# An expert layer's down matrices issued by ScalarE's DMA queue, the gate/up matrices by SyncE's

## The chip, the cores and the metric

The kernel runs on one core of one Trainium2 chip, in float32 throughout. The metric is the device time of one launch in microseconds (us). The engines are TensorE (PE; PEld is its weight load), VectorE (DVE), ScalarE (ACT), GpSimd (POOL) and SyncE (SP, which here only issues DMAs). All DMAs of the core run on its 16 DMA engines; the profile tells them apart by queue: q1 is SyncE's, q10 ScalarE's, q0 GpSimd's.

## What is computed

One decoder layer on 1024 tokens of width 1024: three token mixers, a norm, then a mixture of 64 experts (each token goes to 8 of them) with one shared expert and a per-layer embedding, then a last norm. The change lies in the routed experts, which the reference writes as

```python
def swiglu(x, w_gu, w_down):
    gate, up = jnp.split(x @ w_gu, 2, axis=-1)
    return (jax.nn.silu(gate) * up) @ w_down

def block(acc, inp):
    tok, wt, ex = inp
    y = swiglu(x_pad[tok], w_gu[ex], w_down[ex])
    return acc.at[tok].add((y * wt[:, None]).astype(acc.dtype)), None
```

`w_gu[ex]` is 1024 x 512 (2 MB), `w_down[ex]` is 256 x 1024 (1 MB). `tok` are the tokens routed to the expert.

## The kernel before

The experts are sorted by load, and the 63 most loaded ones get one *place* each (NS = 63; the rest goes through a spill loop at the end). Table `rank_e`, computed on the chip, says which expert stands at a place. A place holds 128 rows (a **single**) or more, up to 216 (a **double**, whose rows above 128 are a second block); in `PLACES` doubles and singles mostly take turns, 34 and 29 of them. `chunks(r)` counts the blocks ahead of place r.

What happens for place r, by engine:

- GpSimd (L3392 to L3402): in turn r it gathers the rows of place r (4 DMAs for the first block, one for each 32 rows of the second, and one of gates for each block; helper line L3343), then issues the adds of place r - 4 (`add_place`, L3359): an indirect DMA for each block that adds the output rows into `acc_scratch` in HBM. An add waits until all adds of earlier places have landed (x_out). A gather waits for the transpose (x_xt) and the gate columns (x_gate) of the places up to two back.
- VectorE (L3260 to L3277): transposes the gathered rows (L3175), multiplies gate and up (L3269, L3272), writes one half of the output (L3237, or L3231 for a second block of at most 32 rows) and copies the gate columns (L3245, L3248).
- TensorE (L2703 to L2727): `hidden(r + 1)`, the gate/up product (L2647 for a double, L2690 for a single), comes before the down product of place r (L2655, and L2662 or L2670 for a second block). A single also has its hidden block turned (L2697), one place before its down product.
- ScalarE (L2832 to L2848): the Silu of place r (L2841), the outputs of place r - 1 (`y_half`, L2821 and L2823), and for a single the copy of the turned hidden block (L2848), on which its down product waits.
- SyncE (L2420 to L2423): the weight loads. `gu` and `dn` are rings of RING = 5 buffers each. `gate_up_in(r)` waits until place r - 5's gate/up product is done (x_u), `down_in(r)` until place r - 5's down product is (x_dn). Both look the expert up with `table`, which reads it into a register. All stand in one queue, in program order:

```python
for r in range(3, NS):
    gate_up_in(r)
    if r >= 4:
        down_in(r)
```

`outputs(r)` needs the adds of place r - 2 landed, since `yoA` and `yoB` have two buffers each. The down product of place r + 1 needs the outputs of place r, since both use the same PSUM banks.

Of the kernel before, what the change touches and what calls it, by code (L numbers as in the profile page):

```python
# [24 lines left out]
NE = 64  # L25
# [3 lines left out]
RING = 5  # L29
# [64 lines left out]
def place_rows(q):  # L94

    return rank_rows(PLACES[q])
# [74 lines left out]
def build(nc, a, out):  # L171

    ctx = ExitStack()
    with ctx:
        stage_sems = []

        def sem(name):
            stage_sems.append(nc.alloc_semaphore(name=name))
            return stage_sems[-1]
# [16 lines left out]
        def carve(n, at=None):  # L196
            at0 = top[0] if at is None else at
            if at is None:
                top[0] += n
            assert at0 + n <= ARENA, (at0, n)  # L200
            return A[:, at0:at0 + n]
# [1897 lines left out]
        with nc.Block() as block:  # L2099
# [25 lines left out]
            def _(pool):  # L2125
# [10 lines left out]
            rank_e = take(NE).bitcast(I32)  # L2136
# [54 lines left out]
                  for x, at in ((1, E_SPILL), (2, E_SPILL + 4 * CQ), (4, R3 + 4 * HALF))}  # L2191
# [3 lines left out]
            NS = NE - 1  # L2195
            gu = [carve(GU, at).rearrange("p (k n) -> p k n", k=KD) for at in (E_GU, base, base + GU, hT_at, hT_at + GU)]
            dn = [carve(DN, at).rearrange("p (f n) -> p f n", f=2) for at in [E_GU + GU] + [AC + i * DN for i in range(RING - 1)]]
# [27 lines left out]
            e_par, e_lg, e_sc, e_chain, e_g, e_st, e_msk, e_tot, e_cnt, e_rank, e_cap, e_cols, e_rows, e_tab, e_pos = (  # L2225
                sem("e_" + n) for n in ("par", "logits", "scores", "chain", "gates", "store", "mask", "totals", "count", "rank",
                                        "capacity", "cols", "rows", "tables", "pos"))
# [27 lines left out]
            x_wg, x_wd = ([sem(f"x_w{n}{i}") for i in range(RING)] for n in "gd")  # L2255
# [27 lines left out]
            dn_v = a["exp_w_down"].rearrange("e (f p) n -> e p f n", p=P)  # L2283
# [13 lines left out]
            def more(r):  # L2297
                return place_rows(r) - P
# [11 lines left out]
            def chunks(r):  # L2310

                return sum(2 if more(q) else 1 for q in range(r))

            def pair(r):
                return 2 * (r % 3)

            def singles(r):

                return sum(not more(q) for q in range(r))

            def table(eng, ap, i, most):
                return eng.value_load(ap[0:1, bass.ds(i, 1)], min_val=0, max_val=most)

            def n_spills(eng):
                return eng.value_load(spills[0:1, 0:1], min_val=1, max_val=OVB)
# [14 lines left out]
            def _(sp):  # L2340
# [38 lines left out]
                def gate_up_in(r):  # L2379
                    e = table(sp, rank_e, r, NE - 1)  # L2380
                    if r == 0:
                        sp.wait_ge(f_dn, 2 * NT)
                    elif r == 1:
                        sp.wait_ge(f_p7, 7 * PPAIRS)
                    elif r < RING:
                        sp.wait_ge(f_p7, 7 * PU)
                        if r >= 3:
                            sp.wait_ge(f_sg, KEPT)
                    else:
                        sp.wait_ge(x_u, r - RING + 1)  # L2390
                    sp.dma_start(two_rows(gu[r % RING]), gu_v[bass.ds(e, 1)].rearrange("a p c two n -> p (a c) (two n)")).then_inc(x_wg[r % RING], 16)

                def down_in(r):
                    e = table(sp, rank_e, r, NE - 1)
                    if 0 < r < RING:
                        sp.wait_ge(f_st[r - 1], 32)
                    elif r:
                        sp.wait_ge(x_dn, chunks(r - RING + 1))
                    sp.dma_start(dn[r % RING], dn_v[bass.ds(e, 1)].rearrange("a p f n -> p (a f) n")).then_inc(x_wd[r % RING], 16)
# [19 lines left out]
                        down_in(t // 2)  # L2419
                for r in range(3, NS):  # L2420
                    gate_up_in(r)
                    if r >= 4:
                        down_in(r)  # L2423
                sp.wait_ge(x_u, NS - RING + 1)
                sp.dma_start(n_g, row("ln2_g", 0, D)).then_inc(n_par, 16)
# [3 lines left out]
                n = n_spills(sp)  # L2429
                with sp.Fori(0, n) as j:  # L2430
                    e = table(sp, spill_e, j, NE - 1)
# [333 lines left out]
            def _(act):  # L2765
# [28 lines left out]
                for q in range(4):  # L2794
                    half, f = q // 2, q % 2
# [20 lines left out]
                def y_half(r, out, gate, n, c, bank):  # L2816
                    act.wait_ge(x_gate, c + 1)
                    if r >= 2:
                        act.wait_ge(x_out, 16 * chunks(r - 1))
                    act.wait_ge(x_dn, c + 1)  # L2820
                    last = nc.scalar.activation(out[r % 2][0:n, 0:HALF], PS[0:n, bank, :], ACT.Copy, scale=gate[r % 2][0:n, :])  # L2821
                    if n <= 32:
                        last = nc.scalar.activation(out[r % 2][0:n, HALF:2 * HALF], PS[64:64 + n, bank, :], ACT.Copy,  # L2823
                                                    scale=gate[r % 2][0:n, :])
                    last.then_inc(x_ya, 1)

                def outputs(r):
                    y_half(r, yoA, gateA, P, chunks(r), 6)
                    if more(r):
                        y_half(r, yoB, gateB, more(r), chunks(r) + 1, pair(r))  # L2830

                for r in range(NS):  # L2832
                    n = place_rows(r)
                    if more(r):
                        act.wait_ge(x_g, r + 1 - singles(r))
                    else:
                        act.wait_ge(x_u, r + 1)
                    if r >= 2:
                        act.wait_ge(x_hid, r - 1)
                        act.wait_ge(x_ht, singles(r - 1))  # L2840
                    nc.scalar.activation(sl[r % 2][:, 0:2 * n], PS[:, pair(r), 0:2 * n], ACT.Silu).then_inc(x_sl, 1)  # L2841
                    if r:
                        outputs(r - 1)
                    if not more(r):
                        act.wait_ge(x_ht, singles(r) + 1)
                        if r >= 2:
                            act.wait_ge(x_dn, chunks(r - 1))
                        nc.scalar.activation(hidT[r % 2][:, 0:2 * P], PS[:, pair(r) + 1, 0:2 * P], ACT.Copy).then_inc(x_hc, 1)  # L2848
                outputs(NS - 1)
                n = n_spills(act)  # L2850
# [641 lines left out]
```

## Time and profile before

| | |
|---|---|
| median of 3 runs | 2307.42 us (2306.7 to 2308.29) |
| profiled execution, its own time | 2311.8 us |
| its span, first to last instruction | 2310.0 us |
| TensorE busy | 2243.6 us, 97% |
| VectorE, ScalarE, GpSimd busy | 1165.2, 459.6, 757.2 us |
| mean granted clock of TensorE | 0.992 |
| DMA | 386.12 MB, mean 167 GB/s; 345 to 361 GB/s in the expert stage |

The span is what lies between the first and the last instruction; 1.8 us of the execution's own time lie around it. The expert stage takes the last third, from about 1440 to 2270. A busy share says how much of the time an engine had work in hand. For TensorE it counts matmuls whose ends are modelled, so a wait can be larger than the gaps that it leaves. A DMA share near or above 1 says that packets were always under way on all 16 engines.

### The profile page before, as it was taken

Reading aid. Unit: us, or ns where it says so; the run is one execution under the profiler, and the core shown is the slowest. Engines: PE = TensorE matmul, PEld = TensorE weight load, DVE = VectorE, ACT = ScalarE, POOL = GpSimd, SP = SyncE. Lnnn points to the kernel's source line nnn. Section 1 sums busy time; section 2 is a strip of 40 time slices with the busy share of each in tenths; the row PEclk is TensorE's granted clock in tenths of the full one; section 3 lists DMA queues with packets and bytes.
Section 4 is the critical chain, followed back from the end, with each engine's and each line's share of the span. In section 5 each row is a group of like instructions: output and inputs, shape, how many; then the busy total and the mean of one; then the engine's idle time right before and its main releaser. Section 6 shows DMA issues by size and latency. Waiting matters only on the chain. (4 is left out here: it accounts for less than half of the span.)

```text
span 2310.0 us, 26726 instructions
## 1 busy us (share of the span) xinstructions
PE 2243.6 (97%) x9622; PEld 1314.9 (57%) x9622; DVE 1165.2 (50%) x2023; ACT 459.6 (20%) x778; POOL 757.2 (33%) x755
## 2 busy tenths in 40 slices
PE   8999999999999999999999999999999999999985
PEld 4784554445795444444445567665656666566552
DVE  6643886786757454554585556323223222232324
ACT  3001114665441111011102100111111111111113
POOL 1000110002531000000000056567777677776652
PEclk9999999999999999999999999999999999999998
DMA  7212011113001111101322320899999999999985
GB/s 295 79 38 72 3 35 60 49 43 110 2 30 64 55 61 58 55 28 55 148 98 99 134 74 1 308 361 358 355 354 358 346 345 349 350 349 347 346 236 179
DMA packets 142389, 386.12 MB, mean 167 GB/s; under 512 B 22508, under 2 KB 51424, under 8 KB 141234
## 3 DMA queue, kind: packets, MB, share of 16 engines
q1 hardware_dynamic: 110242, 307.49, 36.0%
q0 software_dynamic: 30976, 70.08, 12.0%
q10 hardware_dynamic: 1040, 6.83, 0.7%
q8 instruction: 78, 1.28, 0.2%
q14 instruction: 53, 0.43, 0.1%
HBM read 328.30 MB, written 66.58 MB: 171 GB/s over the span
## 5 line engine op out<-in xcount | busy, mean ns | idle before, releaser
L3343 POOL DMA_INDIRECT arena<-hp_scratch,arena x300 | 305.4, 1018 | 143.0 <-issue 85.3
L2647 PE MATMUL banks<-arena 128*128 128x136 f32 (+8 forms) x2240 | 305.7, 297 | 2.7 <-DVE arena L3286 1.9
L2647 PEld LDWEIGHTS banks<-arena 128*128 128x128 f32 x2240 | 301.3, 190 | 6.1 <-issue 3.9
L1887 PE MATMUL banks<-arena 128*128 128x512 f32 x672 | 290.8, 592 | 2.5 <-DVE arena L2020 1.5
L2655 PE MATMUL banks<-arena 128*128 128x512 f32 (+1 forms) x528 | 238.9, 595 | 5.6 <-ACT arena L2848 4.7
L1887 PEld LDWEIGHTS banks<-arena 128*128 128x128 f32 x672 | 127.2, 190 | 163.0 <-issue 162.5
L2690 PE MATMUL banks<-arena 128*128 128x512 f32 x464 | 204.8, 593 | 0.0
L3237 DVE TENSOR_SCALAR arena<-banks,arena 128x512 f32<-128x512 f32 (+4 forms) x75 | 56.3, 751 | 289.1 <-DMA acc_scratch<-arena 247.5
L285 POOL TENSOR_SCALAR arena<-arena 128x1 f32<-128x1 f32 x16 | 4.9, 307 | 567.6 <-DVE arena L276 567.6
L3359 POOL DMA_INDIRECT acc_scratch<-arena x97 | 150.4, 1551 | 81.1 <-DMA acc_scratch<-arena 39.5
L3175 DVE STREAM_TRANSPOSE arena<-arena 128x1024 f32<-128x1024 f32 (+3 forms) x97 | 96.7, 1001 | 156.5 <-DMA arena<-gt_scratch,arena 156.0
L2655 PEld LDWEIGHTS banks<-arena 128*128 128x128 f32 (+1 forms) x528 | 97.9, 189 | 117.2 <-issue 111.0
L2821 ACT ACTIVATE arena<-banks,arena 128x512 f32<-128x512 f32 (+7 forms) x97 | 62.8, 680 | 491.1 <-DMA acc_scratch<-arena 402.8
L1131 PE MATMUL banks<-arena 128*128 128x512 f32 x336 | 150.7, 604 | 3.7 <-ACT arena L1346 3.7
L2690 PEld LDWEIGHTS banks<-arena 128*128 128x128 f32 x464 | 87.4, 189 | 113.6 <-issue 113.6
L1899 PE MATMUL banks<-arena 128*128 128x512 f32 x336 | 146.3, 592 | 0.0
L449 PE MATMUL banks<-arena 128*128 128x256 f32 (+1 forms) x560 | 145.1, 421 | 0.0
L2031 DVE TENSOR_TENSOR arena<-arena,banks 128x512 f32<-128x512 f32 x84 | 56.5, 687 | 164.3 <-PE banks L1887 164.3
L449 PEld LDWEIGHTS banks<-arena 128*128 128x128 f32 x560 | 106.0, 189 | 39.0 <-issue 26.8
L1131 PEld LDWEIGHTS banks<-arena 128*128 128x128 f32 x336 | 63.8, 193 | 88.7 <-issue 83.1
L1899 PEld LDWEIGHTS banks<-arena 128*128 128x128 f32 x336 | 63.6, 189 | 80.7 <-issue 80.7
L3343 POOL DMA_INDIRECT arena<-gt_scratch,arena x98 | 96.0, 979 | 29.9 <-issue 24.7
(477 smaller groups left out, 2983.1 us busy)
## 6 DMA issues: line engine op xcount, KB each, us to landing
arena<-in_exp_w_gu SPq DMA_DIRECT2D x64, 2048.0 KB, 30.2
arena<-in_exp_w_down SPq DMA_DIRECT2D x64, 1024.0 KB, 26.3
arena<-in_w_in SPq DMA_DIRECT2D x20, 1024.0 KB, 5.4
arena<-in_w_in SPq DMA_DIRECT2D x6, 2048.0 KB, 8.5
arena<-in_w_branch SPq DMA_DIRECT2D x12, 512.0 KB, 6.5
arena<-in_ple_w_g SPq DMA_DIRECT2D x3, 2048.0 KB
hp_scratch<-arena SPq DMA_DIRECT2D x10, 512.0 KB, 3.3
acc_scratch<-arena SPq DMA_DIRECT2D x10, 512.0 KB, 4.6
```

Source lines behind the costliest of these rows:

```text
L449: last = nc.tensor.matmul(PS[:, 4 + n % 4, 0:width], lhs(k), rhs(k), start=(k == 0), stop=(k == 3))
L1131: last = nc.tensor.matmul(PS[:, q_bank(n), :], w[:, k, :], tok[:, k, :], start=(k == 0), stop=(k == 3))
L1887: last = nc.tensor.matmul(PS[:, g % 4, :], lhs[:, k, :], rhs[:, k, :], start=(k == 0), stop=(k == 3))
L1899: last = nc.tensor.matmul(PS[:, 4 + g % 4, :], lhs[:, k, :], rhs[:, k, :], start=(k == 0), stop=(k == 1))
L2031: nc.vector.tensor_tensor(dst, src, PS[:, (7 * i + idx) % 4, :], ALU.add).then_inc(m_dve, 1)
L2647: last = nc.tensor.matmul(PS[:, bank + part, f * n:(f + 1) * n], weights[:, k, part * FF + f * P:part * FF + (f + 1) * P], x[:, k, 0:n], s ...
L2655: last = nc.tensor.matmul(PS[0:n, bank + j, :], hid[:, f, lo:lo + n], weights[:, f, j * HALF:(j + 1) * HALF], start=(f == 0), stop=(f == 1))
L2690: last = nc.tensor.matmul(PS[:, pair(r), :], x[:, k, :], gu[r % RING][:, k, :], start=(k == 0), stop=(k == KD - 1))
L2821: last = nc.scalar.activation(out[r % 2][0:n, 0:HALF], PS[0:n, bank, :], ACT.Copy, scale=gate[r % 2][0:n, :])
L3175: nc.vector.transpose(x, src).then_inc(x_xt, 1)
L3343: nc.gpsimd.indirect_dma_start(out=rows[0:n, :], out_offset=None, in_=table, in_offset=bass.IndirectOffsetOnAxis(ap=at, axis=0), bounds_ch ...
L3359: nc.gpsimd.indirect_dma_start(out=acc_d, out_offset=bass.IndirectOffsetOnAxis(ap=slot_i[0:n, block:block + 1], axis=0), in_=rows[0:n, :], ...
```

## The change

SyncE keeps the down loads of the first five places. From place 5 on each is issued by ScalarE, right after it has written its part of the outputs of place r - 5 (whose down product is the last reader of the buffer), with a look-up and a wait of its own on the same count x_dn. The gate/up loads stay where they are. Buffers, sizes, semaphores and what TensorE waits for are unchanged.

```diff
                 for r in range(3, NS):
                     gate_up_in(r)
-                    if r >= 4:
+                    if r == 4:
                         down_in(r)
...
+                def down_in(r):
+                    e = table(act, rank_e, r, NE - 1)
+                    act.wait_ge(x_dn, chunks(r - RING + 1))
+                    act.dma_start(dn[r % RING], dn_v[bass.ds(e, 1)].rearrange("a p f n -> p (a f) n")).then_inc(x_wd[r % RING], 16)
+
+                act.wait_ge(e_tab, 1)
                 for r in range(NS):
...
                     nc.scalar.activation(sl[r % 2][:, 0:2 * n], PS[:, pair(r), 0:2 * n], ACT.Silu).then_inc(x_sl, 1)
                     if r:
                         outputs(r - 1)
+                        if r - 1 + RING < NS:
+                            down_in(r - 1 + RING)
                     if not more(r):
                         act.wait_ge(x_ht, singles(r) + 1)
```

## Rows read from the trace of the kernel before

**Rows 1.** Windows of the expert stage: us, busy us of each engine, PEclk, DMA share, GB/s.

```profile
1480.00:1860.00 380.00, 380.00 (x1702) 244.88 (x1702) 107.15 (x177) 51.93 (x97) 264.11 (x239) 1.00 1.03 358
1860.00:2240.00 380.00, 376.28 (x1743) 237.24 (x1741) 111.89 (x189) 56.18 (x107) 263.49 (x236) 1.00 1.01 339
```

**Rows 2.** TensorE's waits, 1440 to 2270: who waited for whom, us, times, longest.

```profile
PE banks L2655 <- ACT arena L2848: 4.7, 2, 4.5
PE banks L2697 <- DVE arena L3272: 3.6, 3, 2.4
```

**Rows 3.** Chain of waits, 2028 to 2130, shares of that stretch by line.

```profile
by line: DMA acc_scratch<-arena 70.9%; issue 18.3%; POOL arena L3343 10.3%; POOL acc_scratch L3359 4.3%; DVE arena L3237 1.5%; POOLq L3343 0.4%; POOLq L3359 0.3%; DVE arena L3248 0.1%; POOLq L3372 0.1%; DVE arena L3245 0.1%; DVEq L3245 0.1%
```

**Rows 4.** Timeline of GpSimd, 2060 to 2130: start, us, what, [idle before <-releaser].

```profile
2076.37 1.64 POOL L3359 DMA_INDIRECT acc_scratch<-arena  x1 [0.30 <-issue]
2078.31 1.35 POOL L3359 DMA_INDIRECT acc_scratch<-arena  x1 [0.31 <-issue]
...
2087.28 1.62 POOL L3359 DMA_INDIRECT acc_scratch<-arena  x1 [0.99 <-DMA acc_scratch<-arena]
2091.47 1.04 POOL L3343 DMA_INDIRECT arena<-hp_scratch,arena  x1 [2.57 <-DVE arena L3248]
...
2100.54 1.63 POOL L3359 DMA_INDIRECT acc_scratch<-arena  x1 [0.30 <-issue]
```

**Rows 5.** Timeline of VectorE, two stretches: 1795 to 1840 and 2060 to 2130.

```profile
1829.34 0.75 DVE L3237 TENSOR_SCALAR arena<-banks,arena 128x512 f32<-128x512 f32 x1 [3.04 <-PE banks L2655]
...
2086.52 0.75 DVE L3237 TENSOR_SCALAR arena<-banks,arena 128x512 f32<-128x512 f32 x1 [5.18 <-DMA acc_scratch<-arena]
...
2096.49 0.75 DVE L3237 TENSOR_SCALAR arena<-banks,arena 128x512 f32<-128x512 f32 x1 [4.12 <-DMA acc_scratch<-arena]
```

**Rows 6.** Timeline of TensorE and ScalarE around 1836 and 2090.

```profile
1835.91 3.59 PE L2655 MATMUL banks<-arena 128*128 128x512 f32 x8
...
2083.00 8.01 PE L2647 MATMUL banks<-arena 128*128 128x144 f32 x64
2090.84 3.60 PE L2655 MATMUL banks<-arena 128*128 128x512 f32 x8
...
2106.33 8.87 PE L2647 MATMUL banks<-arena 128*128 128x160 f32 x64
...
2088.54 0.38 ACT L2848 ACTIVATE arena<-banks 128x256 f32<-128x256 f32 x1
...
2096.54 0.69 ACT L2821 ACTIVATE arena<-banks,arena 128x512 f32<-128x512 f32 x1 [7.32 <-DMA acc_scratch<-arena]
```

**Rows 7.** Timeline of SyncE's queue around 1560, 2063 and 2083.

```profile
1560.43 0.38 SPq L2399 DMA_DIRECT2D arena<-in_exp_w_down  x1
1561.58 0.38 SPq L2391 DMA_DIRECT2D arena<-in_exp_w_gu  x1
...
2063.52 3.51 SPq L2391 DMA_DIRECT2D arena<-in_exp_w_gu  x1
...
2083.00 4.77 SPq L2399 DMA_DIRECT2D arena<-in_exp_w_down  x1
```

**Rows 8.** Line L2391, all 63 gate/up loads, us from issue to landing.

```profile
DMA to landing us min/median/max: 9.3/30.2/33.0
```

**Rows 9.** ScalarE's earlier DMA L1956, and its queue's packets from 859.4 to 861.9.

```profile
L1956 ACTq DMA_DIRECT2D arena<-y_lru_scratch x1: 403/403/403, 859.5 to 859.5; - x1
...
q10 hardware_dynamic: 3, 0.05, 5.2%
```

**Rows 10.** DMA queues from 2081.2 to 2085: packets, MB, share of 16 engines.

```profile
q0 software_dynamic: 125, 0.51, 67.2%
q1 hardware_dynamic: 138, 0.54, 37.3%
```

**Rows 11.** DMA queues from 14.6 to 19.0.

```profile
q1 hardware_dynamic: 236, 0.90, 52.0%
q10 hardware_dynamic: 235, 0.90, 50.6%
```

## The prediction, made before the changed kernel was run

> **What bounds the kernel now.** I read the page first: TensorE is busy 97% of the span, and over its last 820 us the DMA row stands at 9. That is the stage of the 63 expert places, which the change touches. The windows [rows 1] show both limits at once: of the 760 us from 1480 to 2240 TensorE is busy 756.3, and the DMA share is 1.03, then 1.01. Nothing here has room, and little can be won: the stage's waits [rows 2] hold 4.7 us before L2655 and 3.6 us before L2697 that came through ScalarE or VectorE, 8.3 us in all.
>
> Next, who is nearest behind TensorE. In the chain of waits of a late stretch [rows 3] 70.9% is the landing of the adds into acc_scratch and no weight load appears. So I took one turn of that loop apart [rows 4, 5]. The adds of a double place are issued at 2076.37 and 2078.31; 8.2 us after the second, at 2086.52, they have landed and the outputs of two places later may be written; at 2091.47, the gate columns ready, the next double's seven gathers begin; then the next double's add goes out at 2100.54. One turn (two places) lasts 24.17 us. TensorE itself, from one double's first matmul to the next one's, needs 23.3, from 2083.00 to 2106.33 [rows 6]. In this late part the loop is the slower of the two, and hardly hidden. At 1829.34 VectorE's output waited for TensorE and not for an add [rows 5], so up to there TensorE set the pace. The single place's add between (2087.28, landed 2096.49) has 4.05 us to spare before 2100.54.
>
> The weights are not late: the gate/up load issued at 2063.52 (place 52) lands at most 33.0 us later, 2096.5 [rows 7, 8], and its first matmul runs at 2106.33 [rows 6]: 9.8 us to spare. Down matrices have more.
>
> **The change, part by part.**
> *ScalarE gains 58 issues* (places 5 to 62). Each is a table load into a register, a wait and a DMA. SP shows the load's price: the down issue ends at 1560.81, the gate/up issue starts at 1561.58 with its wait long met, 0.77 us; the issue takes 0.38 when the queue has room [rows 7], and ScalarE's own earlier one took 0.40 [rows 9]. Together 1.15 us, 67 us over the stage, on an engine busy some 14% of it [rows 1]. The wait (x_dn) has been met by the outputs just before, so it costs nothing and nothing new queues behind it. What stands behind the issue is the copy L2848 for a single place and the Silu L2841. The copy ended at 2088.92 and its matmuls began at 2090.84 [rows 6]: 1.9 us of cover, 0.8 after. Not on the path: 0. Without that cover it is 1.15 us each time. On SP an issue took 4.77 us at 2083.00 [rows 7], late in the stage, where at 1560 it took 0.38: I read this as a queue with loads piled up in it. ScalarE's queue would hold one or two loads of 1 MB, so I take 0.38; the ends are 0.37 and 4.8.
>
> *SP loses the same 58* and with them the wait for the down product before each gate/up load, which can then be issued some 4 to 6 us earlier (a down product, 3.6 us, and an issue). It lands 9.8 us early already: 0. The buffers, bytes and other queues' orders stay.
>
> *The down loads move to a third queue.* This is the part that counts. Where adds and SP's queue are both at work [rows 10] they carry 125 and 138 packets: they alternate. By their shares an add packet takes 3.8 x 16 x 0.672 / 125 = 0.327 us and a weight packet 0.164. In the one dense stretch where SP's and ScalarE's queues are both full [rows 11] it is 236 to 235. So I expect three queues to alternate too, which no stretch of this trace shows. A block of 128 rows gives each of the 16 engines 8 add packets: 8 x 0.491 = 3.9 us now, 8 x 0.655 = 5.2 us beside two weight queues, **1.3 us more**, 1.5 with the second block's one or two packets. That is the upper end for one landing; the lower is 0, if they never meet. (The Trainium skill, DMA: Bandwidth & Descriptors, section on queues, rings and completion order, says that each engine goes round-robin between the queue rows that have work, a packet at a time. It speaks against this change: two full weight rows leave the adds a third. For two rows the trace agrees.)
>
> When do they meet? ScalarE ends the single place's output at 2097.2, loads and issues until 2098.4; data started 2.4 us after ScalarE's earlier issue (three packets by 861.9) [rows 9], so at about 2100.4. 1 MB is 16 packets for each engine: 5.2 us beside SP's queue, some 6.6 with the gathers' packets between, so until 2107. The double's adds issued at 2076.37 were moving data in 2081.2 to 2085 [rows 10], 4.8 us after the issue; the ones issued at 2100.54 then from 2105.3. They meet for 1.7 us: about one packet less, 0.4 us. The other down load, after the double's output at 2086.5, falls fully on the single's add: 1.3 us of its 4.05 us to spare, but it moves that place's output and so the first load later by 1.3: up to 3 us of meeting, 0.75. I take 0.6 us for each pair of places. From 1829 to 2240 there are 411 / 24.2 = 17 pairs: 17 x 0.6 = **10 us**. Before that TensorE's pace and the loop's own room absorb it.
>
> *Order among the weights.* The down loads, no longer behind 2 MB, land about 15 us earlier against their use; that is 1.2 MB taken from the gate/up loads, which need 2 MB in 12.2 us: some 7 of their 9.8 us to spare. 0, but a bound: with all gone, it costs.
>
> Sum: 2310.0 span + 1.8 around it = 2311.8 for the profiled execution; plus 10 is 2321.8. The median is 4.4 below that execution: **2317.4 us**, own range 2312.5 to 2325.
>
> **Rivals.**
> *A, the full third.* The down loads cover the double's adds wholly (data later than I think, or packets arriving in bunches). Then each pair costs 1.5 us, 26 us from 1829 on, and the loop overtakes TensorE sooner: of the 14 pairs from 1490 to 1829, each with room of its own that no row fixes (between 0 and 1.5 us, I take 0.5), 14 x 1.0 is 14, less 5 us that TensorE can be kept from its outputs before it notices (ready at 1830.1, wanted at 1835.91 [rows 5, 6]): 9 more. 2307.4 + 35 = 2342. For it: rows 10, 11. Against it: the instants above.
> *B, nothing.* The loads fall between the adds, or the engines are so full that it is all one. (The Trainium skill, same page, section "Issuing engines are not separate DMA queues": all queues end on the same 16 engines, and spreading saves only the sequencer's issue time. By that alone the time stays.) 2307.4, within 4.6. For it: bytes are unchanged and SP's issue time was on no path.
> *C, faster.* If SP's queue, rid of a third of its bytes, runs dry while a double's adds move data, they go at 0.327 instead of 0.491 us: 1.3 us less a turn. It decides once gate/up loads land in under some 12 us instead of 30.2 [rows 8]. TensorE then sets the pace and only the waits of rows 2 can be won: 2307.4 - 8.3 = 2299 at best, 2302 likely. Against it: DMA share above 1 [rows 1], and a queue relieved only of what runs beside it.
> *D, ScalarE stalls.* The issue takes 2 to 4.8 us as on SP. From 1.9 us of cover it decides; some 1 us per pair on the way to the single's down product: 2307.4 + 17 = 2324. Against it: a nearly empty queue. That the change does not do what it says I exclude: order and waits are in the code.
>
> **Numbers.** Forecast 0.43, A 0.14, B 0.28, C 0.10, D 0.05. A measurement here can tell 0.2%, 4.6 us, from no change. Slower: forecast, A and D, 0.62, less 0.02 of the forecast's lower edge; same 0.30; faster 0.10. The range 2302 to 2338 leaves out most of A above and half of C below, about 0.18.
>
> **What would show it.** Right: in the changed profile the double's adds land 0.4 to 1.5 us later than 8.2; a turn of the loop lasts 24.7 or more; ScalarE's issues take 0.4 us; gate/up issues on SP short and early, landing near 30 us or later; down loads landing in about 10; TensorE idle some 10 us more. Wrong: adds landing as before (B), waits of TensorE on gate/up loads (their order was worth more than I gave it), or shorter add landings (C).

## The result, and the profile after

| | before | after |
|---|---|---|
| median | 2307.86 us (4 runs, 2306.7 to 2308.95) | 2331.75 us (4 runs, 2328.6 to 2333.51) |
| ratio after / before | | 1.0103, 95% interval 1.0091 to 1.0116 |
| span of the profiled execution | 2310.0 us | 2331.5 us |

The change costs 24 us. The forecast was slower by 10 (2317.4, range 2302 to 2338): the direction and the resource were right, the size was not.

The edit moves the lines below it: L2841 is now L2847, L2848 is L2856, L3175 is L3183, L3237 is L3245, L3272 (a single's multiplication) is L3280, L3343 is L3351, L3359 is L3367. The down loads of ScalarE stand at L2835.

In three of the five series of runs below even the kernel before took 2336 to 2356 us, so each run is compared only with runs of the kernel before from its own series.

**Where the time went.** The expert stage is cut here by places: from the gate/up product of place 5 to that of 25, 41 and 61. The windows of the kernel before (us, PE, PEld, DVE, ACT, POOL busy; then granted clock, DMA share, GB/s):

```profile
1530.70:1780.60 249.90, 249.90 (x1116) 160.49 (x1115) 72.00 (x119) 35.50 (x66) 177.00 (x160) 1.00 1.03 354
1780.60:1974.90 194.30, 193.50 (x904) 122.91 (x903) 57.27 (x95) 27.07 (x52) 140.85 (x127) 1.00 1.03 350
1974.90:2216.60 241.70, 238.78 (x1116) 152.28 (x1115) 72.63 (x123) 37.14 (x70) 169.50 (x153) 1.00 1.01 338
```

and the same places in the changed kernel:

```profile
1529.30:1790.60 261.30, 253.99 (x1117) 163.62 (x1116) 70.87 (x119) 35.02 (x66) 174.54 (x157) 0.99 1.02 345
1790.60:1990.30 199.70, 195.17 (x904) 124.16 (x903) 57.16 (x95) 27.51 (x52) 141.91 (x129) 0.99 1.02 340
1990.30:2238.20 247.90, 239.73 (x1117) 152.32 (x1116) 72.53 (x123) 37.41 (x70) 170.47 (x154) 1.00 0.97 320
```

The three stretches take 261.3, 199.7 and 247.9 us where they took 249.9, 194.3 and 241.7: **11.4, 5.4 and 6.2 us more**, 23.0 in all. The first 20 places, where I had put nothing, pay half. TensorE idles 7.3 us there (261.30 less 253.99) where it idled none.

The loss does not grow evenly inside these stretches. The forecast's own dividing line was 1829, where place 29's product starts. Cut there, before and then after:

```profile
1530.70:1829.00 298.30, 298.30 (x1374) 194.54 (x1373) 86.99 (x144) 42.80 (x80) 212.36 (x192) 1.00 1.03 354
1829.00:2216.60 387.60, 383.88 (x1759) 241.14 (x1758) 114.91 (x193) 56.90 (x108) 274.99 (x247) 1.00 1.01 343
```

```profile
1529.30:1843.50 314.20, 304.03 (x1375) 198.96 (x1374) 85.85 (x144) 42.57 (x80) 212.74 (x192) 0.98 1.02 342
1843.50:2238.20 394.70, 384.86 (x1760) 241.14 (x1759) 114.71 (x193) 57.37 (x108) 274.17 (x247) 1.00 0.99 329
```

It is **15.9 us up to place 29 and 7.1 after it**. Place by place it comes in steps: from place 11 to 27 the start of the product slips by 15.8 us, from place 27 to 40 by nothing (both kernels take the same time for each), and from 40 to 56 by 6.8 more.

**What TensorE waits for.** From 1480 to 2260, the kernel after, us in total, times, longest (before: [rows 2]):

```profile
PE banks L2697 <- DVE arena L3280: 13.5, 9, 3.2
PE banks L2647 <- issue: 4.0, 3, 2.9
PE banks L2655 <- ACT arena L2856: 2.5, 2, 1.3
```

No wait is for a weight load. (The 4.5 us wait of [rows 2] stands at 2244.6, behind the stretches; its like in the kernel after lies beyond 2260.) The largest kind is the turn of a single's hidden block, L2697, which is late because VectorE's multiplication is. The waits put down to "issue" have a cause too: each of the three ends 0.10 us after VectorE has transposed the rows of that product, the longest at 1804.36, so they are waits for late gathers:

```profile
1803.65 0.71 DVE L3183 STREAM_TRANSPOSE arena<-arena 128x512 f32<-128x512 f32 x1 [2.52 <-DMA arena<-gt_scratch,arena]
1804.46 7.77 PE L2647 MATMUL banks<-arena 128*128 128x176 f32 x41 [2.86 <-issue]
```

One step behind, from 1530 to 1790, VectorE's outputs in the kernel before waited for

```profile
DVE arena L3237 <- DMA acc_scratch<-arena: 63.8, 14, 8.0
...
DVE arena L3237 <- PE banks L2655: 21.7, 8, 3.0
```

and in the kernel after for

```profile
DVE arena L3245 <- DMA acc_scratch<-arena: 120.8, 20, 9.2
```

ScalarE's outputs the same: 13 waits for adds and 10 for TensorE's down product before, 20 for adds and none for TensorE after. The outputs, and with them the whole ring of adds and gathers, now run behind the adds from the start.

**One such delay, followed.** GpSimd, VectorE and TensorE of the kernel after around place 10 (start, us, what, idle before):

```profile
1602.74 1.62 POOL L3367 DMA_INDIRECT acc_scratch<-arena  x1 [2.08 <-DMA acc_scratch<-arena]
1604.84 1.04 POOL L3351 DMA_INDIRECT arena<-hp_scratch,arena  x1 [0.47 <-issue]
...
1614.01 0.96 POOL L3351 DMA_INDIRECT arena<-gt_scratch,arena  x1 [0.30 <-issue]
```

```profile
1613.41 0.75 DVE L3245 TENSOR_SCALAR arena<-banks,arena 128x512 f32<-128x512 f32 x1 [5.63 <-DMA acc_scratch<-arena]
...
1621.14 0.71 DVE L3183 STREAM_TRANSPOSE arena<-arena 128x512 f32<-128x512 f32 x1 [2.01 <-DMA arena<-gt_scratch,arena]
1621.77 0.38 DVE L3280 TENSOR_TENSOR arena<-arena,banks 128x256 f32<-128x256 f32 x1
```

```profile
1618.01 1.04 PE L2670 MATMUL banks<-arena 128*8 128x512 f32 x8
1622.21 0.44 PE L2697 MATMUL banks<-arena 128*128 128x128 f32 x2 [3.16 <-DVE arena L3280]
```

The add of the single place 7 had to wait for the adds ahead of it and went out at 1602.74 (in the kernel before, where it waited for no add, at 1598.20). Eight gathers of 1.3 us each stand behind it, the last from 1614.01. VectorE transposes these rows at 1621.14 and multiplies only behind that, so the hidden block is ready at 1622.15, and TensorE has stood still for 3.16 us. The next windows of the same trace:

```profile
1619.00:1622.20 3.20, 0.05 (x4) 0.00 (x0) 1.15 (x3) 0.00 (x0) 2.59 (x3) 1.00 1.05 349
1622.20:1626.20 4.00, 3.99 (x16) 3.99 (x17) 0.00 (x0) 0.00 (x0) 2.48 (x3) 0.60 1.05 313
1626.20:1630.00 3.80, 3.80 (x24) 3.80 (x23) 0.75 (x1) 1.33 (x3) 0.63 (x1) 0.97 0.98 365
```

After the wait the granted clock is 0.60 for 4 us: it fell to half, the 1.2 GHz level, for most of them, and 4 x 0.40 = 1.6 us more are lost. In the expert stage this happens at the waits of 3.16, 2.61 and 2.86 us near 1622, 1714 and 1804, with 0.91 over each 20 us around them, 1.8 us each. A wait of 2.43 us at 2126.2 was followed by 1.00. So places 5 to 24 add up: 7.3 idle + 2 x 1.8 of clock = 10.9 of the 11.4 us.

**Why the adds are late.** The queues while an add of a single place lands, in the kernel before from 1603 to 1607 (packets, MB, share of the 16 engines):

```profile
q0 software_dynamic: 140, 0.53, 64.5%
q1 hardware_dynamic: 157, 0.63, 40.8%
```

and in the kernel after from 1608 to 1612:

```profile
q0 software_dynamic: 114, 0.43, 52.2%
q1 hardware_dynamic: 116, 0.45, 29.4%
q10 hardware_dynamic: 93, 0.37, 22.6%
```

Each engine sends GpSimd's packets at one in 4 x 16 / 140 = 0.457 us before and one in 0.561 after. Eight packets of a block take 3.7 us before and 4.5 after, 0.8 more. The three queues take nearly equal numbers, as the prediction expected of them; it is also what the Trainium skill, DMA: Bandwidth & Descriptors, section on queues, rings and completion order, says of an engine's queue rows.

Over many places: from the start of the issue of a place's last add to the start of the output it holds up (two places later, only where that output waited for it), medians in us:

| kernel | doubles 5-24, 25-40, 41-59 | singles 5-24, 25-40, 41-59 |
|---|---|---|
| before | 8.97, 9.12, 9.24 | 9.44, 9.41, 9.38 |
| after | 9.54, 8.58, 9.53 | 10.62, 9.73, 10.24 |

A single's add is 1.2, 0.3 and 0.9 us later, a double's 0.6, -0.5 and 0.3. (In the kernel before only three outputs waited for a single's add in places 5 to 24.) Over places 25 to 40 the two together are no later than before, and there nothing is lost from place 27 on.

**The loads.** The gate/up loads (L2391) and ScalarE's down loads (L2835) of the kernel after, from issue to landing, and their issues:

```profile
L2391 SPq DMA_DIRECT2D arena<-in_exp_w_gu x63: 372/373/7074, 1356.7 to 2198.8; - x63
...
DMA to landing us min/median/max: 8.9/15.4/41.0
```

```profile
L2835 ACTq DMA_DIRECT2D arena<-in_exp_w_down x7: 379/380/380, 1535.9 to 1614.4; - x7
```

```profile
DMA to landing us min/median/max: 5.2/11.3/14.4
```

The median gate/up load lands in half the time of [rows 8]; the first ones are slower, up to 41. Between landing and first matmul a gate/up matrix now lies ready for a median of 28.6 us in places 5 to 24 and 39.7 from 25 on (before: 17.3, 14.9 and 13.7 in the three parts): once all five buffers are full ahead of TensorE, SyncE's queue is empty part of the time. It starts a packet in 99, 89 and 83% of the half microseconds of the three parts, and both weight queues start one in 76, 50 and 46%.

### The profile page after: what moved, and what is told of

It reads as the page before. It is cut to its first block and busy times, and to the rows that moved or that the text cites. A ratio compares the mean times of both kernels' runs of the same rounds, so it can differ in the third digit from the quotient of the medians.

```text
span 2331.5 us, 26729 instructions
## 1 busy us (share of the span) xinstructions
PE 2251.5 (97%) x9622; PEld 1319.2 (57%) x9622; DVE 1163.9 (50%) x2023; ACT 460.4 (20%) x778; POOL 758.1 (33%) x755
## 5 line engine op out<-in xcount | busy, mean ns | idle before, releaser
L3351 POOL DMA_INDIRECT arena<-hp_scratch,arena x300 | 305.1, 1017 | 146.1 <-issue 84.6
L2647 PE MATMUL banks<-arena 128*128 128x136 f32 (+8 forms) x2240 | 312.5, 301 | 6.7 <-issue 4.0
L2647 PEld LDWEIGHTS banks<-arena 128*128 128x128 f32 x2240 | 307.2, 193 | 11.3 <-issue 8.1
L3245 DVE TENSOR_SCALAR arena<-banks,arena 128x512 f32<-128x512 f32 (+4 forms) x75 | 56.2, 751 | 338.7 <-DMA acc_scratch<-arena 318.7
L3367 POOL DMA_INDIRECT acc_scratch<-arena x97 | 150.4, 1551 | 102.8 <-DMA acc_scratch<-arena 49.8
L3183 DVE STREAM_TRANSPOSE arena<-arena 128x1024 f32<-128x1024 f32 (+3 forms) x97 | 96.5, 1000 | 163.5 <-DMA arena<-gt_scratch,arena 156.5
L3351 POOL DMA_INDIRECT arena<-gt_scratch,arena x98 | 96.0, 980 | 29.9 <-issue 26.8
## 6 DMA issues: line engine op xcount, KB each, us to landing
arena<-in_exp_w_down ACTq DMA_DIRECT2D x58, 1024.0 KB, 11.3
```

What stands on the lines that cost most here:

```text
L2647: last = nc.tensor.matmul(PS[:, bank + part, f * n:(f + 1) * n], weights[:, k, part * FF + f * P:part * FF + (f + 1) * P], x[:, k, 0:n], s ...
L3183: nc.vector.transpose(x, src).then_inc(x_xt, 1)
L3351: nc.gpsimd.indirect_dma_start(out=rows[0:n, :], out_offset=None, in_=table, in_offset=bass.IndirectOffsetOnAxis(ap=at, axis=0), bounds_ch ...
L3367: nc.gpsimd.indirect_dma_start(out=acc_d, out_offset=bass.IndirectOffsetOnAxis(ap=slot_i[0:n, block:block + 1], axis=0), in_=rows[0:n, :], ...
```

## The experiments

**1. Which places pay, and is it ScalarE's time?** The kernel before of this series: median 2308.41. First the look-up and the wait stay on ScalarE, at the 58 places of the change, and all down loads on SyncE (against the kernel before):

```diff
                 for r in range(3, NS):
                     gate_up_in(r)
                     if r >= 4:
                         down_in(r)
...
+                def down_in(r):
+                    e = table(act, rank_e, r, NE - 1)
+                    act.wait_ge(x_dn, chunks(r - RING + 1))
```

> All down loads back on SyncE's queue; ScalarE keeps only the look-up and the wait at the 58 places. Theories: (third queue) the 24 us come from the adds sharing the DMA engines with two full weight queues, so without the third queue 2308 us, adds landing as before. (ScalarE's time) look-up and issue push its copies and outputs back; the look-up is 0.77 of 1.15 us, so about 2308 + 16 = 2324. (order) the gate/up loads go out earlier and the down loads overtake them; neither happens here, so 2308.

Measured: 2308.96, ratio 1.0002 (0.9992 to 1.0011). The look-up and the wait cost nothing.

Then ScalarE issues only the loads of places 5 to 24 (`e_first20`), or only those from 25 on (`e_last38`); SyncE the others.

```diff
-                        if r - 1 + RING < NS:
+                        if r - 1 + RING < NS and (r - 1 + RING < 25):
```

> ScalarE issues the down loads of places 5 to 24 only, SyncE the other 38. In the changed kernel the stretch from place 5 to 25 grew by 11.4 us and the rest by 11.6. (third queue) about 2308 + 12 = 2320, with adds near 10.5 us in the first stretch and back to 9.3 after it. (ScalarE's time) in proportion to 20 of 58 issues: 2308 + 8 = 2316. (order) it is the filling of the rings that counts: the first part alone brings most of it, 2320 or more.

> ScalarE issues the down loads of places 25 to 62, SyncE those before. (third queue) if the price follows from two full queues at once, the catching-up of the down loads only moves to place 25 and on: at least 2308 + 12 = 2320, up to 2330. (ScalarE's time) 38 of 58: 2308 + 16 = 2324. (order) if only the filling at the start mattered, 2308.

Measured: 2319.97, ratio 1.0049 (1.0032 to 1.0066), and 2326.03, ratio 1.0072 (1.0055 to 1.0089). The windows of the first:

```profile
1527.50:1788.60 261.10, 252.50 (x1117) 161.86 (x1116) 71.04 (x119) 35.01 (x66) 175.73 (x158) 0.99 1.02 346
1788.60:1984.30 195.70, 193.69 (x905) 122.74 (x904) 57.18 (x95) 26.91 (x52) 142.20 (x128) 1.00 1.02 344
1984.30:2224.70 240.40, 238.50 (x1116) 152.17 (x1115) 72.82 (x123) 37.18 (x70) 170.88 (x153) 1.00 1.00 335
```

and of the second:

```profile
1529.40:1779.40 250.00, 250.00 (x1117) 160.52 (x1116) 71.58 (x119) 35.21 (x66) 175.80 (x158) 1.00 1.03 355
1779.40:1984.90 205.50, 196.16 (x904) 124.32 (x903) 56.99 (x95) 27.41 (x52) 142.40 (x129) 0.99 1.01 336
1984.90:2232.10 247.20, 239.30 (x1116) 152.21 (x1115) 72.56 (x123) 37.42 (x70) 170.75 (x153) 1.00 0.97 322
```

The places whose loads ScalarE issues pay, the others don't. More is to be seen: places 25 to 40 cost 5.4 us in the changed kernel and 11.2 (205.5 less 194.3) when the third queue begins there. So it is not the early places as such that are dear, but the first ones after the third queue starts. In `e_last38` 11.3 us are lost from place 25 to 38 and nothing from there to 50.

**2. Is it ScalarE's time, or the instant of the load?** The changed kernel with the down load issued ahead of ScalarE's outputs:

```diff
                     if r:
-                        outputs(r - 1)
                         if r - 1 + RING < NS:
                             down_in(r - 1 + RING)
+                        outputs(r - 1)
```

> As the changed kernel, but ScalarE issues the down load ahead of its outputs, as soon as the down product is done, so up to 8 us earlier. (third queue) the down load's packets meet other packets of GpSimd's queue (the gathers, the single's add) and less the double's adds: 2315 to 2332. (ScalarE's time) 1.15 us before each output lies directly in the loop of adds and outputs, 0.6 us more a place at the least: 2345 or more.

Measured in the same series: 2325.44, ratio 1.0071 (1.0054 to 1.0087). If the time of each issue counted, this would be worse than the change, since it now stands ahead of the outputs. The three stretches take 256.1, 200.0 and 243.5, the first and the third less than the changed kernel's. ScalarE's time is not the cause.

**3. A third queue without the weights, and half of the loads each.** `f_small`: all down loads on SyncE, ScalarE issues a store of 512 bytes at the 58 places instead. `f_after_single` and `f_after_double`: ScalarE issues only the loads that follow the outputs of a single, or of a double.

```diff
-                        if r - 1 + RING < NS:
+                        if r - 1 + RING < NS and (not more(r - 1)):
```

> The same kernel as e_small, again, since the chip of that call ran even the kernel before 47 us slower than elsewhere. ScalarE issues a store of 512 bytes in place of each down load. (third queue, by its packets) 2308. (ScalarE's time) up to 2332.

> The same kernel as e_after_single, again: ScalarE issues only the down loads that follow a single's output. (instants decide) 2322 to 2330. (share decides) 2316 to 2321.

> The same kernel as e_after_double, again: ScalarE issues only the down loads that follow a double's output. (instants decide) 2308 to 2314. (share decides) 2316 to 2321.

Measured (kernel before: 2307.63): the store 2309.58, ratio 1.0004 (0.9994 to 1.0013); after singles 2322.49, 1.006 (1.0043 to 1.0077); after doubles 2325.63, 1.0073 (1.0056 to 1.009). So 58 DMAs on a third queue cost nothing that can be told from noise as long as they carry nothing: it is the megabytes on it. The two halves cost 14.9 and 18.0 us, together 33, more than the 24 of the whole and each more than the 2316 to 2321 that I expected of equal halves.

Which add a load delays is as the prediction had it. With loads after singles the doubles' adds are 0.7, 0.4 and -0.5 us later than in the kernel before in the three parts and the singles' 0.0, 0.2 and 0.1; with loads after doubles the doubles' are 0.2, 0.4 and -0.5 later and the singles' 1.4, 1.1 and 0.4. (The doubles' third figure says little: in `e_lookup`, which loses nothing, it is -0.8.) But the singles' adds do not have the 4 us to spare that the prediction gave them: the half that delays them costs at least as much as the other. The stretches take 253.9, 202.0 and 242.6 after singles and 254.1, 202.9 and 244.6 after doubles. The second starts gently and pays most in the middle, which is also where its gate/up lead grows, from 19.7 to 28.5 to 34.9 us (medians of the three parts).

The same three kernels, and that of experiment 4, had run before in a series in which the kernel before took 2355.62:

> Down loads on SyncE's queue; at the same 58 places ScalarE issues a store of 512 bytes on its own queue instead (look-up, wait, issue). It keeps all that the change costs ScalarE and leaves nearly no packets on the third queue. (third queue, by its packets) 2308. (ScalarE's time) the look-up alone was nothing; if the issue is what hurts, up to 2332.

> ScalarE issues only the down loads that follow a single's output, SyncE those that follow a double's. My prediction's instants say that these loads meet the double's adds, which lie in the loop. (instants decide) most of the 24 us: 2322 to 2330. (share decides: what counts is how many bytes the third queue carries beside a full second) half of them: 2316 to 2321.

> The mirror: ScalarE issues only the down loads that follow a double's output, which meet the single's add with 4 us to spare. (instants decide) little: 2308 to 2314. (share decides) half: 2316 to 2321, like the other half.

> The changed kernel, but SyncE issues the gate/up load of place r only when the down load of place r - 1 has landed, so that the two weight queues are less often full together; the gate/up loads' 39 us of lead can pay for it. (third queue: two full weight queues against one of adds) adds nearer 9.3 us, most of the loss gone: 2308 to 2318. (order, lead) the gate/up loads are later than in the changed kernel: no better than 2332.

Measured there: 2364.93, ratio 1.0052 (1.002 to 1.0083); 2355.46, 1.0004 (0.9988 to 1.002); 2355.09, 0.999 (0.9972 to 1.0009); 2358.69, 1.0002 (0.9983 to 1.0021). More on that below.

**4. Does the price depend on both weight queues having a backlog?** The changed kernel, but the gate/up load of place r waits until the down load of place r - 1 has landed. The gate/up loads can't run ahead, and I expected the two weight queues to be full together less often.

```diff
+                        if r > RING:
+                            sp.wait_ge(x_wd[(r - 1) % RING], 16 * ((r - 1) // RING) + 16)
```

> The same kernel as e_in_turn, again: the gate/up load of place r waits for the landing of the down load of place r - 1. (third queue) 2308 to 2318, adds nearer 9.3 us, gate/up lead smaller than in the changed kernel. (order, lead) no better than 2332.

Measured: 2346.33, ratio 1.0164 (1.0147 to 1.0181), 39 us more than before and 15 worse than the change. Its windows:

```profile
1526.90:1788.30 261.40, 253.29 (x1117) 161.84 (x1116) 70.87 (x119) 34.99 (x66) 173.45 (x157) 0.99 0.99 330
1788.30:1995.20 206.90, 195.19 (x905) 122.89 (x904) 56.98 (x95) 27.25 (x52) 143.36 (x129) 1.00 0.98 329
1995.20:2249.30 254.10, 242.30 (x1117) 153.88 (x1116) 72.36 (x123) 37.37 (x70) 170.03 (x154) 0.99 0.98 327
```

and TensorE's waits from 1480 to 2260 (its lines stand two further on):

```profile
PE banks L2699 <- DVE arena L3282: 15.8, 14, 2.5
PE banks L2649 <- issue: 6.6, 3, 3.5
PE banks L2657 <- ACT arena L2858: 6.6, 7, 1.7
```

Still nothing waits for weights, but now every stretch costs 11 to 13 us, where the change costs 11.4, then 5.4 and 6.2. The gate/up lead stays at some 17 us, and the outputs get their adds 10.62, 10.14 and 10.23 us (doubles) and 11.2, 10.71 and 10.81 us (singles) after the issue. I had tried it to take the loss away; it holds the loss at its early height.

Is the price set by how long both weight queues have work? In the changed kernel it falls as that share falls, but over three kernels the two do not go together (share of half microseconds in which both weight queues start a packet, and us lost, in the three parts):

| kernel | both start packets | us lost |
|---|---|---|
| changed | 76, 50, 46% | 11.4, 5.4, 6.2 |
| load ahead of outputs (experiment 2) | 63, 61, 58% | 6.2, 5.7, 1.8 |
| in turn | 57, 48, 52% | 11.5, 12.6, 12.4 |

What goes with the price is how late the adds are (with the load ahead of the outputs 9.4, 8.4 and 8.9 us for doubles, 9.8, 9.7 and 9.6 for singles), and a long common backlog is not all that makes them late. Why they are latest here stays open.

**5. Order, lead and bytes.** Two series (kernel before 2335.72 and 2354.16). `gate_first`: the kernel before, one queue, with the gate/up load of place r + 1 ahead of the down load of place r.

```diff
-                    if r >= 4:
-                        down_in(r)
+                    if r >= 5:
+                        down_in(r - 1)
+                down_in(NS - 1)
```

> The kernel before, all loads in SyncE's queue, but the gate/up load of place r + 1 is issued ahead of the down load of place r, so it no longer waits for a down product. (order) if freeing the gate/up loads is what lets the weights run ahead and hurts, 2320. (third queue) the one queue still alternates one to one with the adds: 2308.

> The kernel before, with the one queue's order changed: the gate/up matrix of place r+1 goes ahead of the down matrix of place r (gate_first once more, beside the kernel before on the same chip). Order theory (the cost of the first 20 places is that the down matrices run ahead of the gate/up ones): 2315 to 2320 us, places 5 to 24 in 255 to 261 us. Third-queue theory (the cost is two weight queues moving at once beside GpSimd's): within 3 us of the kernel before, places 5 to 24 in 249 to 252 us.

Measured: 2334.88, ratio 0.9998 (0.9988 to 1.0008), and 2348.72, 0.9969 (0.9946 to 0.9992). The lead of gate/up is the changed kernel's there (medians 30.1, 40.3 and 39.0 us in the first) with no loss. By the times alone that says little, since in the series at 2355.62 variants of the change lost nothing either. The adds say more: in that series those of `e_in_turn` were nearly as late as those of `f_in_turn` (doubles 10.7, 10.0 and 9.6 us, singles 11.3, 10.8 and 10.7), while with `gate_first` the doubles' come after 8.9, 9.4 and 8.8 us, about as in the kernel before. So the order and a long lead by themselves do not delay the adds. The small gain of the second series (0.3%) did not show in the first.

`short_lead`: the changed kernel, each gate/up load waits for the product of place r - 3 instead of r - 5.

```diff
-                        sp.wait_ge(x_u, r - RING + 1)
+                        sp.wait_ge(x_u, r - RING + 3)
```

> The changed kernel with the gate/up loads held back two places (they wait for the product of place r - 3), which keeps their lead near 15 us instead of 39, so nothing is there to fill. (filling) the loss of the first 20 places goes, that of the rest stays: about 2308 + 12 + 5 = 2325 or less. (third queue alone, wherever both weight queues are busy) 2332 or more, as in f_in_turn, whose lead was as short.

Measured: 2342.62, ratio 1.0036 (1.002 to 1.0052). The lead fell to some 15 us, but the changed kernel was not in this series, so whether the loss grew or shrank by it is not shown. `half_before` and `half_after`: both kernels with only half of each gate/up matrix loaded (left out: a third of the weights' bytes).

> The kernel before, each gate/up load of the 63 places cut to the first half of its rows, a third of the weight bytes left out (the products use what the buffer held). The DMA engines have room then. (all) adds may land sooner; TensorE sets the pace: 2296 to 2306.

> The changed kernel with the same half gate/up loads, a third of the weight bytes left out. (third queue, which needs both weight queues full while adds move) the loss is gone: within 3 us of g_half_before. (anything that does not depend on full DMA engines: look-ups, waits, completion of a third queue) 10 to 24 us above g_half_before.

> The changed kernel with its gate/up loads cut to half (leaves out half of each gate/up matrix, so a third of the weights' bytes). Third-queue theory (GpSimd's adds are late where both weight queues have packets to send): both are seldom busy at once, the adds land as before and places 5 to 24 take 249 to 252 us, as in the kernel before, the whole at most 2312 us. ScalarE theory (issuing the loads on ScalarE delays the loop, whatever the bytes): the issues are all still there, so places 5 to 24 take 258 us or more and the whole 2325 us or more. If the whole falls well under 2300 us, the kernel before was bound by bandwidth too.

Measured: 2342.05, ratio 1.0024 (1.0005 to 1.0043); 2341.35, 1.0034 (1.002 to 1.0048); and 2361.98, 1.0035 (1.0015 to 1.0055). With the bytes cut the third queue makes no difference (2341.35 beside 2342.05). But in the series at 2355.62 it made none with all the bytes either (`e_after_single`, `e_after_double`, `e_in_turn`), so these six runs neither bear out nor contradict the backlog. There is no pair with half the bytes from a series at 2308. Both halved kernels even took 6 us more than the kernel before of their series, where I had expected 2 to 12 less of the first; the last section shows what their TensorE did.

## Why the prediction was right and wrong

*The limits, as read from the kernel before: right.* The loop of adds and gathers is next behind TensorE, no weight load is late, and the change works through the adds.

*ScalarE's 58 issues, at nothing: right.* They take 0.38 us each, as taken, and experiments 1 and 2 find no price. *SyncE freed, at nothing: right.* Its issues are short again (median 0.373) and its loads early, on no path.

*Three queues share by packets: right in kind.* Forecast 1.3 us more for a landing that is wholly met; the single at 1608 shows 0.8, and medians of singles lie 0.3 to 1.2 later.

*0.6 us for each pair, 10 us from 1829 on: the size about right, the form by luck.* Measured 7.1 us over 17 pairs, 0.42 each, but not at a steady price: nothing from place 29 to 40 and nearly all of it from 40 to 56. The instants behind the 0.4 and 0.75 did say rightly which add is delayed (experiment 3), but not the price of it: the single's add was given 4.05 us to spare and a delay of it costs as much as one of the double's.

*"Before that TensorE's pace and the loop's own room absorb it": wrong, and this is the whole miss.* Forecast 0 up to 1829, measured 15.9 (the late part came out 2.9 under its 10). Two things were in it. First, room: I had judged from one output, at 1829.34, that waited for TensorE and not for an add [rows 5]. Over places 5 to 24 the view of the waits has 14 of VectorE's outputs waiting for adds against 8 for TensorE, in the kernel before. The loop was level with TensorE there and not behind it, and the rival of a full third, which gave each early pair 0.5 us of room and then 9 us of loss in all, was nearer. Second, the size: I took one meeting time for the whole stage, from the rows near 2090. In the early places the adds are delayed more than that, a double's by 0.6 us and a single's by 1.2, and TensorE loses 15.8 us over the 11 pairs of places 5 to 26, 1.4 a pair. Experiment 1 moves this dear start to place 25 and experiment 4 makes its price last.

*The clock was not in the sum.* At each of the three longest waits (2.61 to 3.16 us) TensorE ran 3 to 4 us at 1.2 GHz, 1.8 us a time, 5.4 us of the 23; all three lie in the early part.

*The rivals.* A (full third) 2342: 9 us forecast up to 1829, 15.9 measured; 26 forecast after it, 7.1 measured. B (nothing), C (faster) and D (ScalarE stalls) fall: the ratio excludes the first two, ScalarE's issues of 0.38 us and experiments 1 and 2 the last. On B stood a sentence of the Trainium skill (DMA: Bandwidth & Descriptors, "Issuing engines are not separate DMA queues"), that spreading over engines only saves issue time. Here it saved that and cost 24 us, since a queue more also changes the shares.

What remains open is why the adds are delayed most in the first places after the third queue starts. That both weight queues have a backlog there fits experiment 1 and the changed kernel, but not the table of experiment 4, and in no series at 2308 did a kernel send weights over the third queue without a backlog. Also why the two halves of experiment 3 cost more than the whole was not settled; that the weights' lead grows more slowly in each, so that the dear start is longer, would fit, and is not shown.

## What to carry to other kernels

Where the DMA engines are full, a load moved to a second hardware queue is not only issued elsewhere: it takes packets from every other queue, the small latency-bound transfers on GpSimd's first. Before moving one, ask which transfer is on the loop that ends next and what share it keeps. And a cover ("TensorE sets the pace here") is to be counted over all the stretch, by how many waits end on each side, and not read from one instance. A delay comes out in steps, where the cover happens to be used up, and an average price for each turn hides that.

## What the runs showed that I had not expected

- The price of the third queue is not constant: 1.4 us a pair up to place 27, nothing up to place 40, 6.8 us from there to place 56, and 11 to 13 us a stretch where the weight loads wait for each other (`f_in_turn`).
- A stop of TensorE can cost half as much again: 3.2 us idle, then a granted clock of 0.60 over 4 us. It did so at 3.16, 2.86 and 2.61 us in the changed kernel and at 2.14 us in `e_last38` (1934), and not at 2.43 us in the changed kernel (2126).
- What bounds this kernel can change from one series to another. Where the kernel before took 2355.62, its mean granted clock over the runs was 0.987 (0.993 in the series at 2308), and the same kernels that lose 15, 18 and 39 us elsewhere lost nothing. `half_before` (kernel before at 2335.72) shows what stood there instead. TensorE's waits from 1500 to 2240, some of them one by one, and a window:

```profile
PE banks L2647 <- issue: 15.4, 31, 1.7
```

```profile
1654.52 0.28 PE L2647 MATMUL banks<-arena 128*128 128x136 f32 x1 [0.49 <-issue]
1655.25 0.28 PE L2647 MATMUL banks<-arena 128*128 128x136 f32 x1 [0.46 <-issue]
1655.96 0.37 PE L2647 MATMUL banks<-arena 128*128 128x136 f32 x1 [0.44 <-issue]
```

```profile
1798.90:1809.10 10.20, 7.50 (x25) 6.55 (x26) 1.15 (x2) 0.40 (x1) 6.70 (x6) 0.50 0.68 140
```

  These are short waits with no releaser that the profile shows, all 31 between the matmuls of one gate/up product, where the first kernel before has a single wait of 0.8 us, for rows. At four clusters of them, near 1659, 1799, 1942 and 2191, the granted clock goes to 1.2 GHz for 6.8 to 10.2 us, 37.5 us in all; in the first kernel before it is not there once from 1500 to 2240. So TensorE is slower there, and late adds (experiment 5) are hidden: TensorE's waits for VectorE's multiplication came to 5.8 us in `e_in_turn` and to 15.8 in `f_in_turn`. Why those series were like this no run shows.
